# A mixer and retrieval kernel on one core: the last sublayer's attention, output and query projection one tile of rows at a time, the second tile's among the first tile's gathers

## What is computed

```python
def mixer_sublayer(h, w_in, ...):                      # h: 16 meta tokens and 256 rows
    proj = h @ w_in                                    # 2048 -> 7176 columns
    sb_q, sb_k, sb_v, fq, fk, fv, fgate, flogit = split(proj)
    sb = stick_breaking_attention(sb_q, sb_k, sb_v)    # 8 heads of 128, keys s < t
    log_f = log_sigmoid(flogit + b_forget)
    fox = forgetting_attention(rms_norm(fq), rms_norm(fk), fv, log_f)   # 8 heads, s <= t
    merged = concat([rms_norm(sb), rms_norm(fox) * sigmoid(fgate)])
    return merged @ w_out                              # 2048 x 2048

def peer_sublayer(h, w_query, sub_keys, u, v):
    q = (h @ w_query).reshape(rows, 8, 2, 128)         # 2048 x 2048
    s = einsum('thpc,hpnc->thpn', q, sub_keys)         # 128 scores each
    top 16 of each half, top 16 of their 256 sums      # 8 heads x 16 experts a row
    a = gelu(einsum('thkd,td->thk', u[idx], h))        # gather of 2048 columns, dot
    return einsum('thk,thkd->td', softmax(best) * a, v[idx])   # gather, weighted sum
```

## Time and profile before

| | us |
|---|---|
| median of 3 runs | 3127.76 (3127.49 to 3130.35) |
| profiled execution, first to last instruction (span) | 3121.8 |
| end of the first group of projection 4 | 1176 |
| end of projection 4, of projection 5 | 1661, 1756 |
| first gather | 1797.4 |

### The profile page before, as it was taken

How to read it: one execution, slowest core, us unless ns; L and a number is a source line. 1 busy time by engine, 2 the same in 40 slices (tenths; PEclk the granted TensorE clock), 3 DMA queues, 4 the chain that set the end, 5 groups by cost and what they waited for, 6 DMA issues and landing times.

```text
span 3121.8 us, 29077 instructions
## 1 busy us (share of the span) xinstructions
PE 2089.0 (67%) x11378; PEld 1478.6 (47%) x11378; DVE 1836.5 (59%) x2711; ACT 853.8 (27%) x1267; POOL 800.9 (26%) x680
## 2 busy tenths in 40 slices
PE   5888989989999999999999983223232322322235
PEld 2676777888787787666668871000000000000001
DVE  3679886566776664343336697766565555564430
ACT  1334544444454454544545420000000000000000
POOL 1111110000000000000000036665555555555552
PEclk8999999999999999999999996566656566666667
DMA  9887875557665545334226699999999999999998
GB/s 385 289 293 263 296 259 150 184 182 248 210 189 153 164 158 172 111 122 132 85 82 201 194 377 403 422 422 421 421 422 421 422 421 419 421 421 421 421 421 346
DMA packets 244741, 900.90 MB, mean 289 GB/s; under 512 B 20759, under 2 KB 45613, under 8 KB 178413
## 3 DMA queue, kind: packets, MB, share of 16 engines
q0 software_dynamic: 94208, 612.85, 48.9%
q1 hardware_dynamic: 149152, 284.53, 27.8%
q10 hardware_dynamic: 1244, 1.67, 0.2%
HBM read 894.78 MB, written 2.10 MB: 287 GB/s over the span
## 4 chain that ended last, share of the span: by engine, by line
PE 45%; DMA 29%; DVE 10%; ACT 3%; issue 3%; POOL 2%; ACTq 0%; POOLq 0%; DVEq 0%
PE pp L1818 38%; DMA late<-in_peer_v,MI 9%; DMA P<-in_peer_v,MI 5%; PE tp L1818 5%; DMA x<-in_peer_v,MI 5%; DMA ring<-in_peer_v,MI 4%; DVE wL L1130 3%; DMA SY<-in_peer_v,MI 2%; PE tp L1821 2%; ACT wH L626 1%; DMA ring<-in_peer_w_query 1%; DVE UHM L1286 1%; DMA ring<-in_w_in 1%; POOL late L2361 1%; DVE P L1777 0%
## 5 line engine op out<-in xcount | busy, mean ns | idle before, releaser
L1130 DVE TENSOR_TENSOR wL<-ring,wH 128x1024 fp32r<-128x1024 f32 (+3 forms) x504 | 583.2, 1161 | 573.7 <-ACT wH L626 572.4
L1818 PE MATMUL pp<-wH,hH 128*128 128x512 f32 (+3 forms) x1888 | 745.7, 395 | 35.5 <-DVE wL L1130 19.4
L1818 PE MATMUL pp<-wL,hH 128*128 128x512 f32 (+3 forms) x1888 | 721.4, 382 | 0.0
L1818 PE MATMUL pp<-wH,hL 128*128 128x512 f32 (+3 forms) x1888 | 720.5, 382 | 0.0
L626 ACT ACTIVATE wH<-ring 128x1024 fp32r<-128x1024 f32 (+3 forms) x504 | 508.3, 1011 | 729.7 <-PE pp L1818 548.0
L1818 PE MATMUL pp<-late,S 128*32 128x512 f32 x768 | 232.6, 879 | 335.7 <-DMA x<-in_peer_v,MI 156.3
L1818 PEld LDWEIGHTS pp<-wH,hH 128*128 128x128 f32 x1888 | 362.3, 192 | 141.2 <-issue 46.3
L1818 PEld LDWEIGHTS pp<-wH,hL 128*128 128x128 f32 x1888 | 361.6, 192 | 64.1
L1818 PEld LDWEIGHTS pp<-wL,hH 128*128 128x128 f32 x1888 | 362.8, 192 | 57.3 <-issue 1.0
L1777 DVE CUSTOM_DVE_ANT_0 late<-late,P 128x2048 f32<-128x2048 f32 x84 | 191.2, 2288 | 155.2 <-DMA late<-in_peer_u,MI 155.2
L1818 PE MATMUL pp<-P,S 128*32 128x512 f32 x360 | 162.7, 898 | 166.9 <-DMA late<-in_peer_v,MI 93.2
(11 more groups left out here) (305 smaller groups left out, 2985.2 us busy)
## 6 DMA issues: line engine op xcount, KB each, us to landing
ring<-in_w_in SPq DMA_DIRECT2D x288, 512.0 KB, 4.4
ring<-in_w_out SPq DMA_DIRECT2D x96, 512.0 KB, 4.2
P<-in_w_mod POOLq DMA_DIRECT2D x85, 512.0 KB, 5.1
late<-in_w_mod SPq DMA_DIRECT2D x64, 512.0 KB, 9.4
SY<-in_w_mod POOLq DMA_DIRECT2D x43, 512.0 KB, 5.5
ring<-in_w_in SPq DMA_DIRECT2D x48, 368.0 KB, 4.8
ring<-in_peer_w_query SPq DMA_DIRECT2D x32, 512.0 KB, 7.9
ring<-in_w_in SPq DMA_DIRECT2D x24, 344.0 KB, 3.2
```

The source lines that it names most:

```text
L1130: tt(lo, raw, hi.bitcast(F32), ALU.subtract).then_inc(*tick("dve_lo", *names))
L1818: return e.matmul(o, l, r, start=start, stop=stop, skip_group_check=skip)
```

## The change

Projections 5 and 6 become 5 and 6 for tile 0 and 7 and 8 for tile 1, so `w_out_2`, `peer_w_query_2` and the sub-keys are read twice. Their pieces are 128 rows by 1024 columns, not split, and used by plain fp32 matmuls with the transposed activations `hT` as the stationary operand. Queries are stored by rows and turned (`turn_q`). In projection 4, still for both tiles, the forgetting columns come first, then the gates, then the stick-breaking columns; only tile 0's attention is woven in. Tile 1's attention goes into the steps i = 0 (forget rows, head norms), 1 (forgetting) and 2 (stick-breaking), its output and query projection into i = 3, two pieces per dot. `choose(i + 1)` runs on lane M. The gathers of i = 0 begin after tile 0's query projection and use eight slots until the end of projection 8.

```diff
+G_IN2 = cgroups((FG + 688, 1, 344), (FQ, 2, 512), (FK, 2, 512), (FV, 2, 512), (FG, 2, 344), (SQ, 2, 512), (SK, 2, 512),
+                (SV, 2, 512))
+G_OUT2 = [(0, 1024), (1024, 1024)]
+GROUPS = [G_IN, G_OUT, G_IN, G_OUT, G_IN2, G_OUT2, G_OUT2, G_OUT2, G_OUT2]
+BOTH = 5
+NPC = [8] * BOTH + [16] * 4
-NB, NS, NG = 3, 4, 11
-FIRST_DOT = 12
+NB, NS, NG = 3, 4, 13
...
+    def query(p, q):
...
+        if n == 0 and pc == 10:
+            yield "hidden", t
+        if n == 1 and pc == 2:
+            yield "turn_q", p, 0
+        if n == 1 and pc in (4, 6):
+            yield "scores", 4 * t + pc // 2 - 2
+        if n == 1 and pc == 4:
+            yield "open", "M", "choose", 4 * t
...
+    lanes = {(0, 0): (("X", "forget", 1), ("X", "fox_norm", 1, FQ), ("X", "fox_norm", 1, FK)),
+             (1, 0): (("X", "fox", "X", 0, 1), ("Y", "fox", "Y", 1, 1)),
+             (1, 30): (("X", "fox_end", 1),),
+             (2, 0): tuple((lane, stage, lane, half, 1, g) for g in range(2) for stage in ("stick_a", "stick_v")
+                           for lane, half in (("Y", 0), ("X", 1))),
+             (2, 30): (("Y", "stick_norm", 1),)}
+    for i in range(4):
+        if i < 3:
+            yield "open", "M", "choose", i + 1
+        for j in range(32):
+            for name in lanes.get((i, j), ()):
+                yield "open", *name
+            yield "dot", i, j
+            if i and j == 1:
+                yield "blend", i - 1
+            if i and j % 4 == 3:
+                yield "vmix", i - 1, j // 4
+            yield from pump(*((0.45, 0, 0.42), (0.55, 0.55, 0.42), (0.8, 0.8, 0.42), (0, 0, 0.5))[i])
...
+            if i == 3:
+                for _ in range(2):
+                    for event in second:
+                        if event[0] == "beat":
+                            break
+                        yield event
+        yield "drain", *(("X", "Y") if i < 3 else ()), *(("M",) if i < 3 else ())
+        yield "gelu", i
+        if i == 2:
+            yield "swap",
+            for c in (2, 3, 0, 1):
+                yield "chunk", 7, c
+    yield from second
+    yield "rest",
+    yield "drain", "M"
+    for i in range(4, 8):
...
+            had, queue, n = {}, [0, 1, 2, 3, 4, 5, 6, 7], 0
+            for what, *a in order():
+                if what == "swap":
+                    queue = [8, 9, 10] + [i for i in queue if i not in (5, 6, 7)]
+                    BEFORE.update({i: had[i] for i in (5, 6, 7)})
+                if what == "rest":
+                    queue = [5, 6, 7] + [i for i in queue if i != 10]
...
+                if what == "turn_x":
+                    queue = [11, 12] + queue
...
+            def piece_one(p, q):
+                n, c0, wd, pc = PIECES[p][q]
+                r, kk, t = raw_of[p, q], row_of(p, n, pc), tile_of(p)
...
+                w.wait_ge(*at("raw", r))
+                w.wait_ge(*at("chunk", p, kk // 4))
+                for j in range(2):
...
+                    m = mm(o, hT[t][:, kk, :], ring[:, r % NS, 512 * j:512 * j + 512], pc == 0, pc == 15)
...
+            def stick_a(lane, half, t, g):            # PE; hg = 4 >> t heads at a time
...
+                mm(pr[:, 0:512], trl, L, True, t == 0)
+                if t:
+                    mm(pr[:, 0:256], ones, L[:, 256:512], False, True)
...
+            def fox(lane, half, t):                   # PE; nk = 144 + 128 * t
...
+                        mm(pr[:, o:o + nk], ident[0:8, hd:hd + 1].to_broadcast([8, 128]), cumT[:, 0:nk], True, False)
+                        mm(pr[:, o:o + 16], TQ[:, hh, :], mkt[:, 1, hd, :], False, False)
+                        m = mm(pr[:, o + 16:o + nk], TQ[:, hh, :], TK[:, hh, :], False, True)
...
                 if before is not None:
                     w.wait_ge(*at("expert used", before))
-                elif slot in (3, 4):
...
+                elif slot in (0, 1, 2, 3, 7):
+                    w.wait_ge(*at("grouped", 4, 14, 1))
+                elif slot in (4, 5, 6):
+                    w.wait_ge(*at("grouped", 6, 1, 1))
...
+                if slot in (5, 6, 7) and n >= BEFORE["rest"]:
+                    w.wait_ge(*at("grouped", 8, 1))
```

More of the change, by code:

```diff
@@ L323, in order @@
[L323 to L343, removed]
@@ new lines, in queried, with outward @@
+    def queried(p):
+        yield "turn_q", p, 1
+        yield "scores", 4 * tile_of(p) + 2
+        yield "scores", 4 * tile_of(p) + 3
+    def outward(p, q):
+        n, c0, w, pc = PIECES[p][q]
+        if n == 1 and pc in (2, 6):
+            yield "sub_keys", tile_of(p), 2 * pc - 4
+        if n == 1 and pc in (3, 7):
+            yield "chunk", p + 1, pc // 4
+    for p in (5, 6):
+        for q in range(len(PIECES[p])):
+            yield from splits(p, q)
+            yield "piece", p, q
+            if (p, q + 1) in place and p == 5:
+                yield from splits(p, q + 1)
+            if p == 5:
+                yield from attended(q)
+                yield from outward(p, q)
+            else:
+                yield from query(p, q)
+            yield from pump(1, 1, 1)
@@ new lines, in order, with skipping, second_tile @@
+    yield from queried(6)
+    yield "drain", "M"
+    def skipping(events):
+        for event in events:
+            yield event
+            if event[0] in ("chunk", "sub_keys", "turn_q", "scores"):
+                yield "skip_pair",
+    def second_tile():
+        for p in (7, 8):
+            for q in range(len(PIECES[p])):
+                yield from splits(p, q)
+                yield "piece", p, q
+                yield from skipping(outward(p, q) if p == 7 else query(p, q))
+                if p == 7 and q == 4:
+                    yield "late_loads", 1
+                yield "beat",
+        yield from skipping(queried(8))
@@ L353, in order @@
                 yield "blend", i - 1
-            if i > 1 and j % 4 == 3:
+            if j % 4 == 3:
                 yield "vmix", i - 1, j // 4
[L356 to L361, removed]
-        yield "gelu", i
[L363 to L367, removed]
+            yield from pump(0.42, 0, 0)
@@ new lines, in turn_four @@
+                u = next(turn)
+                w.wait_ge(*at("turned", u))
+                if t == 0:
+                    act(mkt[:, 0 if names == "stick" else 1, 4 * half:4 * half + 4, :], heads(tp[u % 2][:, 512:576], 4), ACT.Copy,
+                        scale=kk).then_inc(*tick(R.act))
+                act(R.H[:, 512:1024 + 512 * t], tp[u % 2][:, 0:512 + 512 * t], ACT.Copy, scale=kk).then_inc(
+                    *tick(R.act, ("pair free", u), (names + " keys", *meta)))
+                yield
```

1203 lines of the change are left out of this document (618 added, 585 removed).

## The result

The changed kernel takes 3194.3 us (median of 4 runs, 3191.8 to 3201.2), the kernel before 3127.6 us (4 runs beside it, 3125.2 to 3130.4). The ratio is 1.022, 95% interval 1.020 to 1.024: slower by 67 us, where 11 us less was forecast, and outside the stated range of 3085 to 3157. The profiled execution has a span of 3189.2 us.

What follows compares the result with a forecast made beforehand. TensorE bounds the kernel up to the gathers, DMA behind them: first gather 1677, 1370 us of bytes, 16.3 tail and 47 idle DMA give a span of 3110.6; plus 6.0, time 3116.6 us, range 3085 to 3157.

Steps and rivals of the forecast that it cites:

- Two stages in series, and the sum: Whole kernel: TensorE up to the gathers, then DMA; end is gather start plus bytes at full rate, idle DMA and tail.
- Input projection to 1557: Input projection, split for both tiles with tile 0's attention: 1176 + 330 + 51, ending at 1557 instead of 1661.
- Output projection 67 us: Tile 0's output projection: 56 us of products plus 4, 4 and 3, ending at 1624, where the old stage took 95.
- Query projection to the first gather 53 us: Tile 0's query projection, scores and choice: from 1624 to the first gather at 1677, 120 us earlier than before.
- Step 0, 20 us: First 32 dot gathers: VectorE needs 103 us against 80 of gathers, leaving DMA idle 20 us (12 to 30).
- It just fits if PE is free: Eight slots in steps 1 and 2: 11.9 us against 12.5 per mix; 0.5 us lost each, 8 in all.
- Rival 3: Eight slots don't cover a mix, TensorE late from attention: 2 to 3 us a cycle, 3141 to 3157; chance 0.20.
- PE runs faster when busier: Steps 1 and 2: argument that a busier TensorE runs faster, said against eight slots failing to cover a mix.
- Step 3, 7 us: Tile 1's projections under gathers: VectorE waits for TensorE at two additions to x, 7 us idle DMA (0 to 30).
- Rival 4: TensorE stays at half clock in i = 3: 269 us against 242, 24 more than forecast, 3141; chance 0.08.
- Change of tile, 12 us: From tile 0 to tile 1: first gather waits for choice and query projection, 12 us idle DMA (8 to 25).
- Rival 5: Weights come too slowly in tile 0's two projections: at 2.1 us a piece gathers start 20 us later, 3137; chance 0.08.

Runs made afterwards that it cites:

- early keys: The changed kernel with each half of the sub-keys' load asked for three pieces earlier, transposes left in place: 3164.3 us, ratio 1.011.
- thin run: The kernel before with 8 slots, plus 5 products of constants of 16 columns between the landings of each mix's rows: 3231.6 us, ratio 1.035.
- wide products: The kernel before with 8 slots, plus 5 products of constants of 512 columns between the landings of each mix's rows: 3130.1 us, ratio 1.003.

## Why the prediction was wrong

*Two stages in series, and the sum*: right. Start, bytes at 421.6 GB/s, idle time and tail give the measured span; the bytes (1370 us) were right.

*Input projection to 1557*: it ends at 1573, and the term that was mis-sized is the split pieces, not the attention. Its first group ends at 1180, 4 us behind the landmark taken over from the old trace. Then, each record counted from its start to the next one's, TensorE spends 303.5 us on the split pieces where the sum has 290 (2.72 us a piece), 39 on the meta tokens' matmuls (40), 43 on tile 0's attention, and waits or stands for 7: attention and waits are 50 where the forecast has 51. The old trace, counted the same way, has 311 us of pieces and 113 of attention, so tile 0 keeps 0.38 of the attention's own time. The "remaining 155 us" of the old stage held some 20 us of pieces; that the share of 0.33, taken of it, came out at the right 51 us is luck.

*Output projection 67 us*: 85. The product of 0.88 us was right (with early keys the projection takes 69 us). The step that failed is "the transposes of four chunks and the sub-keys add 4 us": only the instructions were costed, not the landing of a load that is issued at its use. It is 12.4 us of waiting here; the rest of the 16 us that early keys give back is matmuls slower right behind the waits and other waits for weights. In step 3 the same load costs about as much again.

*Query projection to the first gather 53 us*: 52.

*Step 0, 20 us*: 27. VectorE is the bound there, as forecast (91 busy of 106, and 11 of the other 14 are one wait); that its first dot waits for ScalarE behind the last copy was missed, worth 6 to 12.

*"It just fits if PE is free"*, 8 us for eight slots: the step that failed most, 28 us. The comparison was 6.3 + 5.6 = 11.9 against 12.5, for the first gather of the next mix. The loop closes over the fourth: mix + four issues + landing of the fourth, 5.5 + 8.1 + 9.7 us against 19.9 in the cycle shown. Rival 3 had the right consequence (1.8 us a mix, under its 2 to 3, past its turning point of 1.2) with the wrong reason: it had TensorE late because of the attention, and the kernel before with 8 slots, with no attention, loses nearly as much (1.5). "PE runs faster when busier", said against it, is the very cure.

The fixed price of 2.0 us and 436 GB/s of the Trainium skill (DMA: Bandwidth & Descriptors, anatomy of one DMA) was quoted for a margin of 1.8 us; the fourth gather landed 9.7 us after its issue, behind others in the queue, and no margin was there. What the Trainium skill says in TensorE: Matmul & The Clock Gate, section on oscillation, that short bursts between waits for DMA start cold each time, agrees with the thin run (0.85 us apart) and is what the wide products remove.

*Step 3, 7 us*: 23. VectorE does wait for TensorE at two additions to x, as said, for 42 us; the copies of the keys, 46 us more, were not in the sum. With early keys 262 us of this step have 12 us idle. The waits of the changed kernel from 2230 to 2430:

```profile
DVE TAB L1883 <- PE tp L1935: 45.6, 2, 24.8
DVE x L1328 <- PE tp L1932: 41.9, 2, 25.5
```

Rival 4 (half clock) was wrong: the granted clock is 0.89, 0.80 and 1.00 in the three parts of step 3. Its price was also off by its own figures: 269 - 242 is 27 us, of which 7 stood in the forecast already, so 20 us more and not 24.

*Change of tile, 12 us*: 18, within its bounds.

*Rival 5*: waits for weights in tile 0's projections are 4 us in all.

So of the 79 us between forecast and trace (3110.6 and 3189.2) 33 lie before the first gather (4 late at the first group, 12 input projection, 18 output projection, less 1) and 49 behind it (7, 20, 16, 6), less 3 in the tail. The early keys and the clock of the mix, 30 and 26 us when repaired, carry most of what was repairable. The bytes of the second reading were counted rightly; taking them away gives 66 us, and it can't be repaired in this order.

## What to carry to other kernels

When buffers are cut, write the loop for the last transfer of the group that shares them, with every issue in between, and not for the first. When a small load is moved into a ring, ask where it is issued: at its use, its whole landing stands on the engine, and on every in-order engine that waits for that one. And when a short burst of matmuls holds buffers between waits, look at the spacing of its first matmuls: if it is twice that of the last, filler products during the wait may be worth more than buffers.

## What was not expected of the hardware

POOL's issues of gathers are not of one length: 0.94 us mostly, up to 3 us for others (2.44, 2.18, 2.62, 0.94 in the cycle above), so that four issues take 8.1 us. The traces show what lengthens them: a dot that VectorE is running. The dots beside that cycle:

```profile
2306.57 2.29 DVE L1777 CUSTOM_DVE_ANT_0 SY<-SY,P 128x2048 f32<-128x2048 f32 x1 [0.18 <-DMA SY<-in_peer_u,MI]
2307.24 2.44 POOL L2361 DMA_INDIRECT P<-in_peer_v,MI  x1 [7.45 <-PE pp L1818]
...
2309.05 2.29 DVE L1777 CUSTOM_DVE_ANT_0 x<-x,P 128x2048 f32<-128x2048 f32 x1 [0.19 <-DMA x<-in_peer_u,MI]
2309.98 2.18 POOL L2361 DMA_INDIRECT P<-in_peer_v,MI  x1 [0.30 <-issue]
```

The first dot ends at 2308.86, the issue at 2309.68; the second at 2311.34, its issue at 2312.16: 0.82 us behind it both times. In the trace of the changed kernel 176 of the 512 issues begin while a dot runs, and every one ends 0.81 or 0.82 us behind that dot's end; of the other 336, 313 take at most 0.96 us. Between the first and the fourth issue of a mix the 8-slot kernel has 6.4 us on average, where four unhindered ones would have 3 x (0.94 + 0.30) = 3.7. So the dots also lengthen the loop, by an estimated 2.7 us; what placing the issues elsewhere would give no run shows.

And filler products of 512 columns, which double TensorE's busy time (285 to 569 us in 1100), cost the mixes nothing that can be seen, while they turn 389 into 418 GB/s.
